# Gated delta rule: level products on 32x32 tiles of the array for the 32 columns that a level can change

## What is computed

```
lower = jnp.where(strict, jnp.einsum('nbhid,nbhjd->nbhij', kb, k) * decay, 0.0)
a = lower + jnp.eye(CHUNK, dtype=f32)
u = lax.linalg.triangular_solve(a, v * beta[..., None], left_side=True, lower=True, unit_diagonal=True)
w = lax.linalg.triangular_solve(a, kb * jnp.exp(gc)[..., None], left_side=True, lower=True, unit_diagonal=True)
```

## Time and profile before

| | us |
|---|---|
| median of 3 runs | 1729.07 |
| lowest and highest of them | 1727.09, 1729.58 |
| the profiled execution, its own time | 1731.49 |
| its span in the profile | 1729.7 |

### The profile page before, as it was taken

The page is one execution under the profiler, slowest core; times in us unless marked ns, Lnnn a source line. Parts: engine busy times, 40 slices in busy tenths (PEclk is TensorE's granted clock), DMA queues, the critical chain, the costliest instruction groups (busy, mean ns, idle before and its releaser), DMA issues. The chain is left out here.

```text
span 1729.7 us, 40122 instructions
## 1 busy us (share of the span) xinstructions
PE 1637.1 (95%) x17250; PEld 1343.1 (78%) x17250; DVE 1001.0 (58%) x1471; ACT 621.3 (36%) x1260; POOL 924.0 (53%) x854
## 2 busy tenths in 40 slices
PE   4899999989998999999999999998999899999998
PEld 2788999978997655556879999997899765555586
DVE  2664243827774777779238513382777477777911
ACT  4411231124444444455234123112444444445511
POOL 1000389029992587885320047911999358788532
PEclk9899999999999999999999999999999899999999
DMA  9345312210000000113321211231000000010422
GB/s 340 137 159 172 105 32 89 80 62 16 16 4 12 14 13 27 34 36 136 123 89 38 64 39 51 62 102 60 22 17 4 12 14 13 20 40 21 152 95 77
DMA packets 69776, 112.37 MB, mean 65 GB/s; under 512 B 9824, under 2 KB 41824, under 8 KB 69600
## 3 DMA queue, kind: packets, MB, share of 16 engines
q1 hardware_dynamic: 69136, 109.62, 18.8%
q10 hardware_dynamic: 464, 0.17, 0.0%
HBM read 90.30 MB, written 19.47 MB: 63 GB/s over the span
## 5 line engine op out<-in xcount | busy, mean ns | idle before, releaser
L1670 POOL TENSOR_TENSOR attn_accp<-attn_accp,attn_pr 128x1024 f32<-128x1024 f32 x110 | 269.4, 2449 | 42.9 <-ACT attn_pr L1736 37.2
L94 PE MATMUL ps<-in_h_hi,in_w_hi 128*128 128x384 f32 x720 | 244.1, 339 | 2.5 <-DVE in_h_lo L615 2.5
L96 PE MATMUL ps<-in_h_hi,in_w_lo 128*128 128x384 f32 x720 | 242.4, 337 | 0.0
L1940 DVE TENSOR_REDUCE attn_ql<-ps 128x1 f32<-128x1152 f32 x128 | 172.5, 1355 | 102.3 <-PE ps L1858 102.0
L1736 ACT ACTIVATE attn_pr<-ps 128x512 f32<-128x512 f32 x292 | 158.7, 595 | 170.7 <-PE ps L1902 161.8
L1901 PEld LDWEIGHTS ps<-attn_QH,attn_KH 128*128 128x128 f32 x292 | 55.5, 190 | 122.1 <-ACT attn_pr L1736 55.2
L94 PEld LDWEIGHTS ps<-in_h_hi,in_w_hi 128*128 128x128 f32 x720 | 135.7, 188 | 9.3 <-issue 7.5
L1911 PE MATMUL ps<-attn_pr,z 128*64 128x512 f32 x520 | 139.5, 615 | 0.0
L1144 POOL TENSOR_TENSOR delta_ML<-delta_EK,local 128x256 f32<-128x256 f32 x180 | 130.4, 746 | 15.2 <-PE ps L1184 14.5
L96 PEld LDWEIGHTS ps<-in_h_hi,in_w_lo 128*128 128x128 f32 x720 | 135.5, 188 | 0.0
L1901 PE MATMUL ps<-attn_QH,attn_KH 128*128 128x512 f32 x292 | 131.5, 450 | 0.0
(11 more groups left out here) (308 smaller groups left out, 3857.0 us busy)
## 6 DMA issues: line engine op xcount, KB each, us to landing
in_w<-in_w_in SPq DMA_DIRECT2D x21, 1024.0 KB, 5.1
z<-in_w_mod SPq DMA_DIRECT2D x8, 2048.0 KB, 8.0
gates<-in_gate SPq DMA_DIRECT2D x48, 192.0 KB, 1.9
attn_gt<-gates SPq DMA_DIRECT2D x34, 256.0 KB, 2.6
z<-in_x_sample SPq DMA_DIRECT2D x16, 512.0 KB, 6.0
zz<-in_w_mod SPq DMA_DIRECT2D x4, 2048.0 KB, 13.4
out_w<-in_w_out SPq DMA_DIRECT2D x16, 512.0 KB, 5.7
out_y<-z SPq DMA_DIRECT2D x16, 512.0 KB, 2.9
```

The source lines that it names most:

```text
L94: nc.tensor.matmul(out, a_hi(i), b_hi(i), start=(i == 0), stop=False)
L96: last = nc.tensor.matmul(out, a_lo(i), b_hi(i), start=False, stop=(i == n - 1))
L1670: nc.gpsimd.tensor_tensor(acc, a, pr[:, n % 4], ALU.add).then_inc(pool_added, 1)
L1940: nc.vector.tensor_reduce(ql[:, a % 4, blk, HD:HD + 1], ps[:, bank:bank + 3, 0:GRP], AX_XY, ALU.max).then_inc(mx_read, 1)
```

## The change

Levels 1 to 4 stay inside blocks of 32 rows, and a level changes only half of the columns: those of the later block of each pair (of the earlier block, in the transposed form or the other direction). The changed kernel uses both facts.

- `block_products` takes the place of `chunk_products` for levels 1 to 4: 4 heads x 2 chunks x 2 blocks b of 32 rows, each 32 x 32 weights against the 16 columns that can change. It is 32 weight loads and 32 matmuls for one direction in place of 16 and 16; four neighbours in the queue lie on the four diagonal 32x32 tiles of the array.
- `last_level` does level 5: 4 heads x 2 chunks, 32 x 32 weights against 32 columns, off the diagonal of the array. x5 reads `EA` in place of a masked `ML`, so level 5 has no mask on POOL.
- The masks of levels 1 to 4 cover 128 columns in place of 256, and `ML` has a buffer for each level, which POOL zeroes once at the start of a layer; a mask waits for the same level of the last turn.
- The copies to X (128 columns) and the subtractions (128 columns) are half as wide. For x5 ACT makes two copies of 32 partitions in place of one of 128. The transposes L1433 stay 256 columns wide.
- At the start of a layer ACT writes zeros into two PSUM banks, and the first x1 waits for that (`y_zeroed`).

```diff
-        X, ML = both("X", [P, 4, CHUNK]), both("ML", [P, 2, 4, CHUNK])
+        X, ML = both("X", [P, 4, HALF]), both("ML", [P, LEVELS - 2, 4, CHUNK])
...
         def level_mask(i, d):
-            return local[:, L_LEVEL + LEVELS * d + i, :].unsqueeze(1).unsqueeze(1).broadcast_to([P, 2, 2, CHUNK])
+            m, s = CHUNK // 2 ** i, 2 ** i
+            return (local[:, L_LEVEL + LEVELS * d + i, :].rearrange("p (m s) -> p m s", s=s).unsqueeze(1)
+                    .broadcast_to([P, 2, m, s]))
+        def later(x, i, d):
+            return x.rearrange("p (m two s) -> p m two s", two=2, s=2 ** i)[:, :, 1 - d]
+        def earlier(x, i, d):
+            return x.rearrange("p (m two s) -> p m two s", two=2, s=2 ** i)[:, :, d]
...
+                for d in range(2):
+                    nc.gpsimd.memset(ML[d][:], 0.0)
+                pool.drain()
...
                 def mask_level(j, i):
                     for d in range(2):
-                        if i >= 3:
-                            pool.wait_ge(x_mm[d], 5 * j + i - 2)
-                        elif j >= 1:
-                            pool.wait_ge(x_mm[d], 5 * (j - 1) + (5 if i == 1 else 4))
-                        nc.gpsimd.tensor_tensor(pairs(ML[d][:, i % 2]), EA[d][:, j % 3, :, 0], level_mask(i, d),
-                                                ALU.mult).then_inc(ml_done, 1)
+                        if j >= 1:
+                            pool.wait_ge(x_mm[d], 5 * (j - 1) + i)
+                        nc.gpsimd.tensor_tensor(by_pair(later(flat(ML[d][:, i - 1]), i, d)),
+                                                later_pairs(EA[d][:, j % 3, :, 0].rearrange("p a n i -> p a (n i)"), i, d),
+                                                level_mask(i, d), ALU.mult).then_inc(ml_done, 1)
...
                         diagonal(j, d)
-                    mask_level(j, 5)
...
-                def chunk_products(bank, off, lhs, rhs):
+                def block_products(bank, i, lhs, rhs):
                     for h in range(NDH):
                         for c in range(2):
-                            last = nc.tensor.matmul(heads(bank, off)[rows(c), h, :], lhs(rows(c), h), rhs(rows(c), h),
-                                                    start=True, stop=True)
+                            for b in range(2):
+                                r, n = half_rows(c, b), HALF * h + HALF // 2 * b
+                                out = by_block(ps[r, bank, n:n + HALF // 2], i)
+                                last = nc.tensor.matmul(out, lhs(r, h, slice(HALF * b, HALF * b + HALF)),
+                                                        rhs(r, h, b), start=True, stop=True)
+                    return last
+                def last_level(bank, to, lhs, rhs):
+                    for h in range(NDH):
+                        for c in range(2):
+                            last = nc.tensor.matmul(ps[half_rows(c, to), bank, 4 * HALF + HALF * h:5 * HALF + HALF * h],
+                                                    lhs(half_rows(c, 1 - to), h), rhs(half_rows(c, 1 - to), h), start=True, stop=True)
                     return last
...
-                            copy(X[d][:], heads(d), x_out[d])
+                            if name == "x5":
+                                for c in range(2):
+                                    r = half_rows(c, 1 - d)
+                                    last = nc.scalar.activation(X[d][r], ps[r, d, 4 * HALF:8 * HALF]
+                                                                .rearrange("p (h e) -> p h e", e=HALF), ACT.Copy)
+                                last.then_inc(x_out[d], 1)
+                            else:
+                                copy(X[d][:], ps[:, d, 0:4 * HALF].rearrange("p (h e) -> p h e", e=HALF), x_out[d])
...
+                act.wait_ge(pool_out, 6)
+                for d in range(2):
+                    last = nc.scalar.activation(ps[:, 2 + d, 0:8 * HALF], m["masks"][:, 0:2, :].rearrange("p a c -> p (a c)"),
+                                                ACT.Copy, scale=0.0)
+                last.then_inc(y_zeroed, 1)
...
-                            x = TR[d][:, jj, 0 if i < 5 else 1]
-                            nc.vector.tensor_tensor(x, x, heads(2 + d), ALU.subtract).then_inc(y_out[d], 1)
+                            whole = TR[d][:, jj, 0 if i < 5 else 1]
+                            x = earlier(flat(whole), i, d) if i < 5 else later(flat(whole), i, d)
+                            nc.vector.tensor_tensor(x, x, by_block(ps[:, 2 + d, (0 if i < 5 else 4 * HALF):][:, 0:4 * HALF], i),
+                                                    ALU.subtract).then_inc(y_out[d], 1)
                             if i < 5:
                                 dve.wait_ge(y_out[d], 5 * j + i)
-                                nc.vector.transpose(TR[d][:, jj, 1], x).then_inc(r_out[d], 1)
+                                nc.vector.transpose(TR[d][:, jj, 1], whole).then_inc(r_out[d], 1)
```

42 lines of the change are left out of this document (34 added, 8 removed).

## The result

The changed kernel is slower. Its four executions took 1849.5 us in the median (1840.97 to 1853.59), those of the kernel before beside it 1729.3; the ratio is 1.069, with an interval of 1.065 to 1.073. The prediction was 1693, with a range of 1678 to 1722: wrong in sign, and the time lies far outside the range. The profiled execution took 1849.15.

What follows compares the result with a forecast made beforehand. PE, POOL and DVE were seen as close to full, none alone setting the pace, with the turn bound by their chain; 2.02 us less over 18 turns, 36.4 us, took 1729.1 to 1692.7, so 1693, range 1678 to 1722.

Steps and rivals of the forecast that it cites:

- A product in 0.25 us: Level products on PE: one direction's product takes 0.25 us in place of 0.46, bounds 0.21 and 0.48.
- The change of tile size, 0.13: PE between 32x32 and 64x64 products: 0.13 us at each of 12 new places a turn, bounds nothing and 0.2.
- case (b): PE's tile changes: 32 and 64 need no pause between them; turn 13.8 us, time 1685, chance 0.17.
- Subtraction 0.285, copy 0.28, x5's two copies 0.55, mask 0.46: 128-column operations, in us: DVE's subtraction from 0.404, ACT's copies, x5's two 0.17 more than today, POOL's mask from 0.746.
- case (d): POOL's masks: runs of 2 and 4 elements are slow; at 0.95 us a mask, turn 15.05, time 1707, chance 0.07.
- POOL's and DVE's load of a turn, 11.1 and 11.6: Busy time in a turn: POOL falls from 14.91 to 11.1 us, DVE from 12.84 to 11.6.
- PE's 12.8 and POOL's 11.1 fit in.: New turn of 14.25 us: PE's 12.8 and POOL's 11.1 us of work do not limit it; PE is next, 13.7 with waits.
- Does PE take instructions that fast?: PE's issue in level products: 8 ns each needed for 0.25 us at a time; a burst of 8 loads showed 7.
- Case (e): PE's issue: a load and matmul pair needs some 12 to 15 ns; no gain from 0.39 us a product, up to 1763; chance 0.13.
- Case (f): Clock falls as the array does less: turn as long as now at 0.83, 1760 at 0.75; chance 0.07.
- The turn of 14.25: Steady turn from gb to gb: pieces of 8.24 and 6.01 us make 14.25 in place of 16.27, 2.02 less.

Runs made afterwards that it cites:

- e3_wide_moving: Changed kernel with 64 columns moved in x and 32 in y, in place of 16, by the 32x32 products of levels 1 to 4; 1848 us.
- e1: Changed kernel with levels 1 to 4 on 64x64 tiles, 64 columns loaded and 32 moved; 1752 us, ratio 1.014.
- e10: e1 with au placed between x5 and y5 in the order of a turn, in place of behind y5; 1727.1 us, ratio 0.999.
- e5: e1 with level 5 wholly as in before (64x64 tiles, mask, copy and subtraction of 256 columns); 1729.0 us, ratio 0.999.
- e13: e10 with nine unread 128x128 by 256 column products ahead of x1 of a layer's first turn; 1720.1 us, ratio 0.995.
- e12: e5 with au placed between x5 and y5 in the order of a turn; 1726.5 us, ratio 0.999.

## Why the prediction was wrong

The step that failed is the sum that said PE fits in: it priced PE's turn by the time of its loads and left out the time that PE's instructions take to arrive. The prices of single operations were right; the groups of after by line (form, count, busy us, mean ns) answer to the earlier trace rows:

```profile
L1176 POOL TENSOR_TENSOR delta_ML<-delta_EK,local 128x128 f32<-128x128 f32 x144 | 64.1, 471 | 0.0
...
L1497 DVE TENSOR_TENSOR delta_TR<-delta_TR,ps 128x128 f32<-128x128 f32 x180 | 49.3, 274 | 161.2 <-PE ps L1220 130.6 <-PE ps L1228 30.2
L1408 ACT ACTIVATE delta_X<-ps 128x128 f32<-128x128 f32 x144 | 38.3, 277 | 49.1 <-PE ps L1220 44.8
...
L1425 ACT ACTIVATE delta_X<-ps 32x128 f32<-32x128 f32 x72 | 19.3, 268 | 44.0 <-PE ps L1228 42.4
```

- **A product in 0.25 us**: 0.26 where it isn't interrupted (32 loads at 8.3 ns). Right.
- **The change of tile size, 0.13**: 0.17 at 460.78 above, at a full clock. The rule of the Trainium skill that was weighed there ("TensorEngine Tiling (Array Packing)", Tiling Modes (Key Properties)) is borne out for 32 against 64; case (b), no pause, falls.
- **Subtraction 0.285, copy 0.28, x5's two copies 0.55, mask 0.46**: 0.274, 0.277, 2 x 0.268, 0.471. Right; case (d), short runs slow on POOL, falls with the mask.
- **POOL's and DVE's load of a turn, 11.1 and 11.6**: 10.4 and 11.6 in the window above. Near enough.
- **"PE's 12.8 and POOL's 11.1 fit in."** This is the step that failed. PE's load was made up of the loads' time alone, 20 x 0.25 + 6.1 + 1.56 (which is 12.66 and was put down as 12.8). It has a second one that the sum lacks: 1554 instructions at 15.2 ns are 23.6 us, more than the 16.3 of the whole turn before. The question "Does PE take instructions that fast?" was asked, and answered from eight loads in a row, for 0.25 us at a time. At that scale the answer was right, 8.3 ns a load; over a turn it is another resource.
- **Case (e)** came nearest, with the right sign and the right engine. But it put the limit at 12 to 15 ns for a pair within a product. It is 15 ns for each instruction, 30 for a pair, over the turn, so its 1763 and its break-even of 0.39 us a product are both the price of something else: the product stayed at 0.26.
- **Case (f)**, the clock: it fell to 0.64, well under its break-even of 0.83, and yet by e3_wide_moving it cost the changed kernel nothing that can be seen. With the supply out of the way it counts: 1.8 us a turn in e1 against e10 (au's move included), some 3 us in each of e5's first turns.
- **The turn of 14.25** can't be tested with the small tiles. Without them, at a full clock, the same gains of DVE, ACT and POOL, with products of 0.46 us in levels 1 to 4 as before, give 15.1 to 15.9 us (e10), 15.46 in the mean: 0.9 us less than before's 16.36, where 2.02 were forecast with the cheaper products.

A hint stood in the profile before. The earlier trace rows has 505 loads and 507 matmuls in 16.29 us, so PE already took an instruction in 16 ns there, while a steady stream of loads on two tiles takes 29 ns a pair, 14.5 an instruction. Both limits lay side by side at 64 columns, and halving the columns relaxes only one. The two stops of before named above, at 423.41 and 488.99, are rows of before that show how little slack the other had; the prediction did not look at them.

## What to carry to other kernels

Count PE's instructions over a long stretch, not only the time of its loads: here a turn could not be shorter than some 14.7 to 15.7 ns for each load, matmul and wait, and splitting a product into smaller tiles doubles the count for the same work. When work on the array is made smaller, look at what PE does around it: the narrower products lost 1.4% with a clock that fell where the array waited; other work moved into that gap made up for the loss (e10), and nine products ahead of the first turn brought half a percent (e13). An edit that takes time off three engines at no cost to the fourth was worth no more than that here, where the fourth was nearly full.

## What the runs showed of the hardware

- **The supply of PE's instructions**: packets of 16 KB, some 260 instructions, 3.9 to 4.1 us apart in the mean, also while PE stood still for want of instructions. The stops often fall in the middle of a product, last up to 2.5 us and end 2.1 to 3.0 us after a packet; between them the stock goes out at 4 ns an instruction.
- **The clock's return after the idle stretch at a layer's start.** In before it began to return at 386 us, 5 us after the first x1. In e5 it stayed at 0.50 until 399 us, 18 us after the first x1, though PE was busy for 19.61 of the 19.77 us of the turn.
- **DVE kept out by POOL.** In e12's profiled execution (1739.3 us, its slowest) gb's first operation, 128x256 with both operands in SBUF, took up to 5.33 us where its median is 0.67. The window and the timelines of DVE and POOL there:

```profile
448.86:454.20 5.34, 3.38 (x82) 3.12 (x79) 5.34 (x3) 1.75 (x4) 5.05 (x10) 1.00 0.01 3
...
448.86 5.67 DVE L1475 TENSOR_TENSOR delta_D<-delta_GB,cmix 128x256 f32<-128x256 f32 x2
...
451.35 1.20 POOL L1171 TENSOR_TENSOR delta_diag<-local,egl 128x256 f32<-128x256 f32 x2
452.50 1.42 POOL L1181 TENSOR_TENSOR delta_ML<-delta_EK,local 128x256 f32<-128x256 f32 x2
```

POOL works through ten operations back to back, and DVE's ends 0.3 us behind the last of them, at 454.19. PE then waited 3.6 us for DVE, the clock fell, and this turn took 25.0 us, the next 23.9. The Trainium skill ("SBUF — State Buffer", section Terms, shared port pair) describes a port pair that the two engines share, locked for a whole instruction. The trace agrees with the blocking; it shows it over several of POOL's instructions in a row, not one. In the changed kernel the same operation takes up to 2.33 us. That POOL is the cause is read from the times alone; no run was made to separate it.
